# A third query product moved into an expert loop's first steps, and a last norm kept in the layout of its sums

## The reference, cut to what matters

```python
h = layer_norm(DN_ALPHA * h + mix, ln1_g, ln1_b)
q = (h @ w_query).reshape(T, 8, 2, 128)               # 8 heads, 2 halves
s = einsum('thcd,hckd->thck', q, sub_keys)            # 128 scores for each half
s_top, i_top = top_k(s, 16)                           # then the best 16 of 16 x 16 sums
e_idx, g = ...                                        # 16 experts a head, softmax of their scores
hid = gelu(einsum('td,thkd->thk', h, expert_u[e_idx]))
ffn = einsum('thk,thkd->td', g * hid, expert_v[e_idx])
out = layer_norm(DN_ALPHA * h + ffn, ln2_g, ln2_b)
```

## Time and profile before

| | |
|---|---|
| time, median of 3 runs | 913.88 us (913.46 to 914.13) |
| time of the profiled execution | 916.07 us |
| its span, first to last instruction | 914.2 us |
| busy share: TensorE, VectorE, ScalarE, POOL | 80%, 65%, 45%, 33% |
| read from HBM | 330 MB, 268 MB of them by the gathers |
| mean granted TensorE clock | 0.84 of full speed |

### The profile page before, as it was taken

How to read it: one execution, slowest core, us unless ns; L and a number is a source line. 1 busy time by engine, 2 the same in 40 slices (tenths; PEclk the granted TensorE clock), 3 DMA queues, 4 the chain that set the end, 5 groups by cost and what they waited for, 6 DMA issues and landing times.

```text
span 914.2 us, 11720 instructions
## 1 busy us (share of the span) xinstructions
PE 735.0 (80%) x4014; PEld 337.8 (37%) x4016; DVE 596.1 (65%) x1406; ACT 411.9 (45%) x1173; POOL 304.7 (33%) x304
## 2 busy tenths in 40 slices
PE   7999999999959889797797687867666676666664
PEld 6886665656514445342143241413211111101110
DVE  1622861647998878675769576787767666667545
ACT  1144314533588676643344435554343434434333
POOL 0010023002436454523245344344434334344330
PEclk9999999999979799999597878877867656667776
DMA  7633644759999999999999999999999999999993
GB/s 277 251 139 137 223 187 191 312 197 381 385 413 420 398 396 419 422 422 421 416 420 421 422 421 420 420 420 421 421 421 420 422 419 423 420 420 422 421 420 131
DMA packets 47342, 332.21 MB, mean 363 GB/s; under 512 B 6161, under 2 KB 6193, under 8 KB 10545
## 3 DMA queue, kind: packets, MB, share of 16 engines
q0 software_dynamic: 37152, 268.45, 71.0%
q1 hardware_dynamic: 10130, 63.01, 17.8%
HBM read 330.37 MB, written 1.06 MB: 363 GB/s over the span
## 4 chain that ended last, share of the span: by engine, by line
PE 42%; DMA 38%; DVE 10%; ACT 6%; issue 3%; POOL 1%; DVEq 0%; SPq 0%; ACTq 0%; POOLq 0%
DMA late<-in_uv,eidx 22%; DMA ring<-in_uv,eidx 9%; PE ps L1209 9%; DMA wring<-in_uv,eidx 7%; PE ps L781 6%; PE ps L805 6%; PE ps L989 5%; ACT late L1260 3%; PE ps L929 3%; DVE late L2044 3%; PE ps L953 2%; DVE ring L2044 2%; ACT L1260 2%; PE ps L788 2%; PE ps L797 2%
## 5 line engine op out<-in xcount | busy, mean ns | idle before, releaser
L1260 ACT ACTIVATE late<-late 128x1 f32<-128x1 f32 (+3 forms) x787 | 222.3, 285 | 328.6 <-DVE late L2044 306.7
L1209 PE MATMUL ps<-late 64*64 64x512 f32 x976 | 168.4, 780 | 67.6 <-ACT late L1260 67.4
L1209 PE MATMUL ps<-ring,late 64*64 64x512 f32 x912 | 158.7, 784 | 76.4 <-ACT late L1260 76.4
L2044 DVE CUSTOM_DVE_ANT_0 late<-late,x_sb 128x1024 f32<-128x1024 f32 x122 | 149.3, 1224 | 81.9 <-DMA late<-in_uv,eidx 80.9
L2163 POOL DMA_INDIRECT late<-in_uv,eidx x120 | 136.1, 1134 | 176.5 <-PE ps L1209 165.4
L2044 DVE CUSTOM_DVE_ANT_0 ring<-ring,x_sb 128x1024 f32<-128x1024 f32 x114 | 139.5, 1224 | 79.9 <-DMA ring<-in_uv,eidx 79.1
L2163 POOL DMA_INDIRECT ring<-in_uv,eidx x114 | 123.3, 1081 | 173.6 <-PE ps L1209 155.7
L1209 PEld LDWEIGHTS ps<-late 64*64 64x64 f32 x976 | 32.4, 158 | 180.5 <-ACT late L1260 164.5
L1260 ACT ACT_TABLE_LOAD x69 | 88.5, 1283 | 18.8 <-PE ps L781 11.0
L1209 PEld LDWEIGHTS ps<-ring,late 64*64 64x64 f32 x912 | 29.7, 157 | 172.9 <-ACT late L1260 159.7
L1260 ACT ACTIVATE tmp<-ps 128x512 f32<-128x512 f32 (+4 forms) x77 | 37.5, 494 | 66.1 <-PE ps L781 41.2
(11 more groups left out here) (281 smaller groups left out, 796.0 us busy)
## 6 DMA issues: line engine op xcount, KB each, us to landing
wring<-in_wts SPq DMA_DIRECT2D x12, 2048.0 KB, 7.5
kT<-in_wts SPq DMA_DIRECT2D x4, 1024.0 KB
ring<-in_wts SPq DMA_DIRECT2D x3, 1024.0 KB, 10.5
wring<-in_wts SPq DMA_DIRECT2D x2, 1428.0 KB, 5.8
wring<-in_wts SPq DMA_DIRECT2D x2, 1388.0 KB, 6.4
ring<-decay_sums SPq DMA_DIRECT2D x2, 1024.0 KB, 5.7
ring<-in_wts SPq DMA_DIRECT2D x1, 2048.0 KB, 7.2
wkeep<-in_wts SPq DMA_DIRECT2D x1, 2048.0 KB, 13.0
```

Of the source, the lines that this page charges most:

```text
L1209: last = mm(o[t][n * HD:(n + 1) * HD, :], factor[tokens, :], values[tokens, n * 512:(n + 1) * 512], start=start, stop=stop, skip_group_che ...
L1260: return nc.scalar.activation(out, in_, func, **kw)
L2044: V.tensor_tensor_reduce(out=u_row, in0=u_row, in1=h_sb[:, i, :], scale=1.0, scalar=0.0, op0=ALU.mult, op1=ALU.add, accum_out=hdot[:, e, k ...
```

## The change

`EARLY` becomes 2: the query product of head 2 of tile 0 and its scores leave the stretch ahead of the loop. They go where the later heads' are: TensorE does the two halves of the product behind steps 1 and 2 and the scores behind step 6, ScalarE copies the query behind step 5 and the scores behind step 9. ScalarE's copy of these scores behind step 0 goes. The new items of a step stand behind those already there.

The last norm stays in the layout of the sums. The statistics are taken from PSUM for each half of the tokens (64 tokens, half the columns on either group of 64 partitions); 12 numbers a partition cross over, on ScalarE in one direction and on VectorE in the other; then both groups aggregate, and the products read PSUM. The weights are spread in this layout by two pairs of small matmuls and two copies. The output is stored as four pieces of 64 partitions a tile: SP stores columns 0 to 511, ScalarE's queue columns 512 to 1023. At the very end ScalarE does one square root of a constant ahead of the last sums.

```diff
-EARLY = 3
+EARLY = 2
-    put("act", 0, "s", 0, EARLY - 1)
-    for n, k in enumerate((14, 26, 38, 47, 79)):
+    for n, k in enumerate((1, 14, 26, 38, 47, 79)):
         queries(0, EARLY + n, k, 1, 3)
-    for part, k in enumerate((114, 115, 119, 120)):
+    for part, k in enumerate((114, 119)):
         put("pe", k, "ln", part)
         put("act", k + 3, "ln", part)
-    for part in range(2):
-        put("act", 131 + part, "cross", part)
-    put("act", 134, "root", 36, 7)
+    put("act", 132, "cross")
+    put("act", 134, "roots", 48, 7)
+    for t in range(2):
+        put("act", 139, "write", t)
...
             for i in range(NT):
-                for half in range(2):
-                    cols = slice(half * 512, (half + 1) * 512)
-                    sp.wait_ge(out_ready, 2 * i + half + 1)
-                    sp.dma_start(out[i * P:(i + 1) * P, cols], outb[i][:, cols]).then_inc(out_done, 16)
+                for t in range(2):
+                    sp.wait_ge(out_ready, 2 * i + t + 1)
+                    at = i * P + t * HD
+                    sp.dma_start(out[at:at + HD, 0:512], outb[i][0:HD, t, :]).then_inc(out_done, 16)
...
             first_gate(1)
-            for n in range(2, EARLY):
-                query_part(0, n, 0, 1)
-                key_scores(0, n)
...
+            def write_right(i, t):
+                act.wait_ge(out_ready, 2 * i + t + 1)
+                at = i * P + t * HD
+                nc.scalar.dma_start(out[at:at + HD, 512:D], outb[i][HD:P, t, :]).then_inc(out_done, 16)
+
+            def cross(i):
+                act.wait_ge(stats_ready, i + 1)
+                f(groups[HD:P, :, 1, :], groups[0:HD, :, 0, :], ACT.Copy).then_inc(crossed, 1)
...
-            for n in range(2, EARLY):
-                query_copy(0, n)
-                if n < EARLY - 1:
-                    key_scores_copy(0, n)
...
-            for part in range(2):
-                cross(1, part)
-            root(36, 1, 8)
+            f(st[:, 63:64], tri[:, P - 1:P], ACT.Sqrt)
+            cross(1)
+            root(48, 2, 8)
+            for t in range(2):
+                write_right(1, t)
...
             def finish(i, part):
-                if part < 2:
-                    if part == 0:
-                        dve.wait_ge(row_used, STEPS * (i + 1))
-                    same, cols = slice(part * HD, (part + 1) * HD), slice(part * 512, (part + 1) * 512)
-                    link(V.tensor_copy(acc2[same, cols], ps[same, Y_BANK[i] + part, :]))
-                    dve.wait_ge(crossed, 2 * i + part + 1)
-                    statistics(acc2, part, 36)
+                y = [ps[:, Y_BANK[i] + t, :] for t in range(2)]
+                if part == 0:
+                    dve.wait_ge(row_used, STEPS * (i + 1))
+                    for t in range(2):
+                        last = V.bn_stats(groups[:, t, 0, :], y[t])
+                    last.then_inc(stats_ready, 1)
+                elif part == 1:
+                    dve.wait_ge(stats_ready, i + 1)
+                    link(V.tensor_copy(groups[0:HD, :, 1, :], groups[HD:P, :, 0, :]))
+                    dve.wait_ge(crossed, i + 1)
+                    for t in range(2):
+                        last = V.bn_aggr(means[:, t, :], groups[:, t, :, :])
+                    link(last)
+                    V.tensor_scalar(st[:, 52:54], means[:, :, 1], EPS, None, ALU.add).then_inc(ms_ready, 1)
+                elif part == 2:
+                    for n in range(2):
+                        await_taken(dve, "ln", n)
+                    for t in range(2):
+                        last = V.scalar_tensor_tensor(acc2[:, t, :], y[t], means[:, t, 0:1], lnw[:, 0, 0:512], ALU.subtract, ALU.mult)
+                    link(last)
                 else:
-                    layer_norm(outb[i], acc2, acc2, 36, 7 + i, None, part - 2, out_ready)
+                    dve.wait_ge(sd_ready, 7 + i)
+                    link(V.reciprocal(st[:, 60:62], st[:, 56:58]))
+                    for t in range(2):
+                        V.scalar_tensor_tensor(outb[i][:, t, :], acc2[:, t, :], st[:, 60 + t:61 + t], lnw[:, 1, 0:512], ALU.mult, ALU.add).then_inc(out_ready, 1)
```

More of the change, by code:

```diff
@@ L362, in layer @@
         bna = sb("bna", [P, 2])
+        groups = sb("groups", [P, 2, 2, 6])
+        means = sb("means", [P, 2, 2])
         nmx = sb("nmx", [P, 2 * NH])
@@ L469, in layer @@
         wact = view(kv_place[1] + 32, 2, 2, TOPK, src=late)
-        acc2 = view(4096, D)
+        acc2 = view(4096, 2, D // 2)
         last_row = view(0, 2 * D, parts=1)
-        outb = [view(5120, D), view(6144, D)]
+        outb = [view(5120 + i * D, 2, D // 2) for i in range(NT)]
         topi = sb("topi", [P, 2, TOPK], u32)
@@ L567, in layer @@
         crossed = sem("crossed")
+        stats_ready = sem("stats_ready")
         out_ready = sem("out_ready")
@@ L747, in _ @@
             for i in range(NT):
-                for half in range(2):
-                    cols = slice(half * 512, (half + 1) * 512)
-                    sp.wait_ge(out_ready, 2 * i + half + 1)
-                    sp.dma_start(out[i * P:(i + 1) * P, cols], outb[i][:, cols]).then_inc(out_done, 16)
-            sp.wait_ge(out_done, 32 * NT)
+                for t in range(2):
+                    sp.wait_ge(out_ready, 2 * i + t + 1)
+                    at = i * P + t * HD
+                    sp.dma_start(out[at:at + HD, 0:512], outb[i][0:HD, t, :]).then_inc(out_done, 16)
+            sp.wait_ge(out_done, 64 * NT)
         @block.tensor
@@ L1017, in last_norm_rows @@
                 o = await_free(pe, "ln", part)
-                filled(mm(o, tri[0:1, :], last_row[0:1, part * 512:(part + 1) * 512], start=True, stop=True), "ln", part)
+                for n in range(2):
+                    at = (2 * part + n) * 512
+                    last = mm(o[n * HD:(n + 1) * HD, :], tri[0:1, 0:HD], last_row[0:1, at:at + 512], start=True, stop=True)
+                filled(last, "ln", part)
             def token_transposes(i):
@@ L1413, in last_norm_copy @@
                 o = await_full(act, "ln", part)
-                cols = slice(part % 2 * 512, (part % 2 + 1) * 512)
-                taken(f(lnw[:, part // 2, cols], o, ACT.Copy), "ln", part)
+                taken(f(lnw[:, part, 0:512], o, ACT.Copy), "ln", part)
             def hidden_copy():
@@ L1425, in query_copy @@
                 taken(f(qpTs[i][n][:, 0:blocks, :], o[:, 0:blocks * P].rearrange("p (h t) -> p h t", h=blocks), ACT.Copy), "q", i, n)
-            def cross(i, part):
-                if part == 0:
-                    act.wait_ge(row_used, STEPS * (i + 1))
-                there = slice((1 - part) * HD, (2 - part) * HD)
-                f(acc2[there, part * 512:(part + 1) * 512], ps[part * HD:(part + 1) * HD, Y_BANK[i] + 1 - part, :], ACT.Copy).then_inc(crossed, 1)
+            def write_right(i, t):
[5 more added lines that the diff above has]
+                f(groups[HD:P, :, 1, :], groups[0:HD, :, 0, :], ACT.Copy).then_inc(crossed, 1)
             def key_scores_copy(i, n):
@@ L1536, in _ @@
                         root(n[0], 1, n[1])
+                    elif what == "roots":
+                        root(n[0], 2, n[1])
+                    elif what == "write":
+                        write_right(0, *n)
                     elif what == "cross":
-                        cross(0, *n)
+                        cross(0)
                     elif what == "ln":
@@ L1642, in layer_norm @@
                 if part == 0:
[L1643 to L1647, removed]
+                    dve.wait_ge(ln_here, ln_value)
                     for half in range(2):
@@ L2028, in finish @@
             def finish(i, part):
-                if part < 2:
-                    if part == 0:
-                        dve.wait_ge(row_used, STEPS * (i + 1))
-                    same, cols = slice(part * HD, (part + 1) * HD), slice(part * 512, (part + 1) * 512)
-                    link(V.tensor_copy(acc2[same, cols], ps[same, Y_BANK[i] + part, :]))
-                    dve.wait_ge(crossed, 2 * i + part + 1)
-                    statistics(acc2, part, 36)
-                else:
-                    layer_norm(outb[i], acc2, acc2, 36, 7 + i, None, part - 2, out_ready)
+                y = [ps[:, Y_BANK[i] + t, :] for t in range(2)]
[13 more added lines that the diff above has]
+                elif part == 2:
+                    for n in range(2):
+                        await_taken(dve, "ln", n)
+                    for t in range(2):
+                        last = V.scalar_tensor_tensor(acc2[:, t, :], y[t], means[:, t, 0:1], lnw[:, 0, 0:512], ALU.subtract, ALU.mult)
+                    link(last)
+                else:
+                    dve.wait_ge(sd_ready, 7 + i)
+                    link(V.reciprocal(st[:, 60:62], st[:, 56:58]))
+                    for t in range(2):
```

(1 more changed line is left out.)

## The result

The changed kernel takes 918.14 us (median; 917.39 to 920.45), the kernel before 914.13 on the same chip: ratio 1.0048, 95% interval 1.0038 to 1.0058, **slower by 4.0 us** (4.4 by the ratio). The forecast was 917.1. The profiled execution of the changed kernel took 920.0 us with a span of 918.1, the one of before 916.07 with 914.2.

A forecast was written before the change was run, and what follows sets the result against it. DMA bounds the expert loop except near its start, where compute is late. +2.3 us at step 11 (earlier start included), +1.6 clock, -0.7 last norm: +3.2, 917.1 us; range 911.8 to 919.3, slower cases alone 914.9 to 919.3.

The forecast's parts named there:

- What bounds it: Expert loop bound by DMA except near its start; from 262 to 324 compute is late, so delaying step 11 delays the end.
- first hole: DMA dip at 245 to 250, 1.7 us lost; filling it is worth nothing unless compute gets ahead as well.
- The earlier start: Ahead of step 0: without the third query product the first factor is ready 1.5 us earlier, filling most of the hole.
- The wait at step 9: VectorE waits for ScalarE's copy of the third query's scores; step 11's dot product comes 2.3 us later.
- The clock: TensorE idle 3.7 us ahead of step 0, so steps 0 and 1 run at half clock: +1.6 us, between 0 and 3.2.
- rival 4: Two half-clock stretches of TensorE at the loop's start: +4.8 us, 918.7; chance 8%.
- On the way: From step 11 to 324: the chain carries the +3.9 us, with no gain and no loss taken.
- rival 1: TensorE's half-clock stretch from 299.9 to 310.2 regains full clock, at most 4.9 us shorter; 911.4 in the middle; chance 17%.
- second hole: DMA dip at 315 to 325, where row buffers run dry; forecast to come later by about 4 us.
- The last norm: At the kernel's end: statistics and products read PSUM, 0.7 us saved, bounds 0 and 1.1.
- rival 3: Last norm does not end sooner, ScalarE's stores starting slowly or the crossing costing more: +3.9 us, 917.8; chance 10%.
- Tile 0's norm: Steps 132 to 139, where DMA runs at 420 GB/s with the buffers full: priced at nothing.

The follow-up runs named there:

- e11: Changed kernel with the choice of head 2's experts one step later and 32 unread matmuls ahead of the loop: 912.82 us, 0.9984 of the kernel before.
- e1: Kernel before with the new last norm alone, the loop's start as before: 915.15 us, 1.0007 of the kernel before.
- e3: Changed kernel with the copy of the third query's scores put ahead of squares, table load and exponentials in ScalarE's step 9: 915.98 us, ratio 1.0021.
- e6: Changed kernel with VectorE's choice of head 2's experts one step later, from step 9 to step 10: 914.08 us, 0.9998 of the kernel before.
- e5: Changed kernel with 32 matmuls that nothing reads (3.7 us of TensorE) ahead of the loop: 917.49 us, 1.0033 of the kernel before.
- e12: Changed kernel with head 2's choice one step later, 32 unread matmuls ahead of the loop and one 128-partition store per half tile: 928.35 us, ratio 1.0150.
- e10: Changed kernel with head 2's choice one step later and one store over 128 partitions per half tile: 930.63 us, 1.0177 of the kernel before.
- e2: Kernel before with the third query product moved behind steps 1 and 2, the last norm as before: 918.94 us, 1.0055 of the kernel before.
- e7: Changed kernel with head 2's choice one step later and the scores' copy first in ScalarE's step 9: 915.11 us, 1.0002 of the kernel before.
- e4: Changed kernel with 64 unread matmuls (7.3 us, twice as long as meant) ahead of the loop: 919.06 us, 1.0054 of the kernel before.
- e8: e1 (new last norm alone) with all four stores of a tile from SP: 915.16 us, 1.0006 of the kernel before.
- e9: e1 (new last norm alone) with one store over all 128 partitions for each half of the tokens: 931.95 us, 1.0192 of the kernel before.

## Why the prediction was right

**What bounds it: right in the main.** POOL issues its last gather 4.2 us later (890.29 for 886.12), the last sum comes 4.2 us later, and the DMA holes add up to that within about a microsecond. Whatever delayed step 11 delayed the end. That a filled first hole is worth nothing unless compute gets ahead looks too strong: e11 gains on e1 with step 11 no earlier.

**The earlier start: right.** From the Silu's start to step 0 it is 3.42 us (239.37 to 242.79) where it was 4.93 (238.75 to 243.68): 1.5 earlier, as forecast. The first hole shrank by 1.0.

**The wait at step 9: right in place and size.** From the dot product of step 9 to the choice I had 5.5 us; it is 5.4 (256.40 to 261.82). e3 and e6 show that the time hangs on it. Net of the earlier start I gave it +2.3, so 3.8 gross: putting the choice behind step 10 moved step 11 by 3.3 us, counted from the Silu, and the time by 4.6 by the ratios (e6).

**The clock: right, and the size is shown at its place; that it came out at 1.6 is in part luck.** 16 matmuls lost 1.64 us at half clock, forecast 1.6, and e5 gave 1.65 back at the compressed scores. But the size varies. Counted from the Silu's start, the compressed scores begin at 12.2 us in the three executions with e5's filler (e5, e11, e12), at 13.6 to 13.8 in four without it (the changed kernel, e3, e6, e10), and at 14.9 in two (e2, e7), where the half clock went on into the first half of the query product. So the loss is 1.4 to 1.7 us or 2.7 to 2.8; the second is rival 4's mechanism, a longer half clock at the start, which I had priced at 3.2. In the time the three pairs with and without the filler give 1.4, 1.3 and 2.5 us; the forecast lies between them. Step 11 came 4.0 us later by the trace, 3.9 forecast; 0.6 of the 4.0 is this execution's later arrival at the loop.

**On the way: the terms that I set to nothing were two, and they partly cancelled.** The half-clock stretch behind 300 became shorter and gave back 1.4 us (+3.9 at 304.36, +2.5 at 325.06). That is rival 1's mechanism, at less than a third of its size (4.9). Then the new stretch at 354.81 came ahead of a hole that costs 2.3; that the stretch caused it is argued from the order in the trace. Where such stretches fall differs: e2, with the same start, loses nothing between 365 and 385 and is as slow. The length of an idle time alone didn't decide it either: in the trace of before, the 8 matmuls at 384.28 took 1.09 us, full clock, behind 3.97 us idle. My argument that this hardly varies, from three runs within 0.7 us, was too weak: in later runs the kernel before took 911.71 to 917.28 in 22 of 23 executions. The new hole at 275 to 285 and the second hole's delay came as described.

**The last norm: the sum was nearly right, two of its terms were not.** On VectorE I forecast 0.7 saved; it is 1.3. The two statistics took 1.30 together, not 1.46; from their end to the aggregates 0.34, not 0.4; two aggregates 0.28, not 0.45; and the products that read PSUM took 1.41, no more than the 1.42 on SBUF. Against that the stores lost 1.0 us, which I had only as a bound ("0, ScalarE's DMA issue slower than SP's"). (The 0.99 us that I read as SP's two issues holds the wait between them; each takes 0.33.) Net, the trace has 0.3, and e1 nothing that can be measured. So rival 3's price (+3.9) is the nearer one for this term, though its reason is only half of it: the cut into halves of 64 partitions costs 1.5 us, and the second queue wins 0.5 back. The rule cited in the prediction, that two transfers to disjoint halves gain nothing against one, agrees with the trace: cut in halves the stores ended 1.0 us later. What in the cut costs this wasn't separated.

**Tile 0's norm: nothing, as priced.** In e1 the windows from 600 to 640, where its norm and stores lie, are all at 417 to 422 GB/s.

With the terms as measured, 4.2 us at the last sum less 0.3 at the end make 3.9, the difference of the two spans; the medians are 4.0 apart. My 3.2 was low by the norm's 0.4 and, in this execution, by what the stretches on the way took net of a step 11 that came 0.5 us less late than forecast; that these partly cancelled was luck. The 914.9 that the prediction gives for the slower cases doesn't follow from it: beyond 1.8 us they begin at 915.7.

## What to carry to other kernels

An item moved between the steps of a loop can cost what is queued behind the first engine that waits for its result. Here that was VectorE, not TensorE, which did the moved work. Ask for each moved result who reads it first and behind what its producer now stands; moving that reader one step on gave the whole 4 us back. And when work leaves an engine ahead of a loop, look at the idle time that it leaves: TensorE's next 16 matmuls ran at half clock, and products that nothing reads were cheaper than the gap as long as they ended before step 0 could start (e5, e11), and not when they were twice as long (e4).

## What the runs showed of the hardware

- Statistics, aggregates and products that read PSUM were not slower here than on SBUF: 0.65 us each for two 128x512 statistics (0.69 from SBUF before), 1.41 for two products (1.42).
- A store over 64 partitions takes SP longer to issue than one over 128: 0.47 us alone and 0.60 when issued in a row (e8), 0.33 before. The stores of e9, over 128 partitions with the destination in two blocks, took 0.51 and more.
- A store over 128 partitions whose destination is two blocks of 64 rows ran at a DMA share of 0.13 and about 50 GB/s; with four such stores e9 was 17 us slower than the kernel before.
- Behind the same 3.80 us idle, TensorE's next 16 matmuls took 3.3 us in e6 and 3.7 in e2, and the 16 after them 2.05 and 3.10; with the idle time filled (0.23 us left in e5) the clock stayed full.
